# Loads of x asked for earlier, and a scheduling model with two kinds of DMA queue, in a hybrid decoder layer

## What is computed

```python
h = x
h = h + parallel_mixer(rms_norm(h, mix_norm_g), ...)          # this stage is where the change lies
h = h + memory_cross_attention(rms_norm(h, cross_norm_g), ...) # 4 heads into 256 memory tokens
h = h + swiglu_ffn(rms_norm(h, ffn_norm_g), ...)               # width 2816
# in parallel_mixer
proj = xn @ w_in                                   # 1024 -> 3072
q, k, v, u = split(proj, [1536, 2048, 2560])       # q: 3 groups x 4 heads x 128; k, v, u: 512 each
q = rope_partial(rms_norm(q), cos, sin) * 128 ** -0.5
k = rope_partial(rms_norm(k), cos, sin)
# three dilated windows (128/1, 512/4, 2048/16) of q over k, v, merged by their denominators;
# u: causal means over 2, 4, 8, 16 positions minus the token, a linear map a group;
# both concatenated @ w_out
```

## Time and profile before

| | |
|---|---|
| median of three runs | 1014.95 us |
| profiled execution | 1013.88 us |
| its slowest core (core 1), first to last instruction | 1012.3 us |
| spans of cores 0 to 7 | 1008.2, 1012.3, 1011.8, 1004.5, 1005.1, 1010.1, 998.9, 1011.2 us |
| granted TensorE clock of cores 0 to 7, mean share | 0.991, 0.993, 0.993, 0.993, 0.995, 0.991, 0.998, 0.993 |
| PE busy on core 1 | 953.9 us, 94% of the span |
| DVE, ACT, POOL busy | 446.1, 386.1, 170.5 us |
| chain that ended last | 88% PE, 4% DMA, 2% DVE, 2% ACT |

### The profile page before, as it was taken

How to read it: one execution, slowest core, us unless ns; L and a number is a source line. 1 busy time by engine, 2 the same in 40 slices (tenths; PEclk the granted TensorE clock), 3 DMA queues, 4 the chain that set the end, 5 groups by cost and what they waited for, 6 DMA issues and landing times.

```text
span 1012.3 us, 16727 instructions; the slowest of 8 cores (998.9 to 1012.3 us)
## 1 busy us (share of the span) xinstructions
PE 953.9 (94%) x5716; PEld 474.3 (47%) x5716; DVE 446.1 (44%) x970; ACT 386.1 (38%) x726; POOL 170.5 (17%) x253
## 2 busy tenths in 40 slices
PE   1789999999998799989999999999999999999998
PEld 1345545555556575434443444444444444444443
DVE  2437793666774457656787221122261212211111
ACT  2436656555558785436784111112110111111000
POOL 1214453333340002111220000010110000010000
PEclk9989999999999999999999999999999999999999
DMA  9876434020039779400220345448476255539471
GB/s 220 207 139 162 116 54 77 14 51 12 11 101 182 226 214 194 114 0 1 37 48 1 47 79 84 84 74 125 97 130 138 42 84 84 83 61 138 80 143 59
DMA packets 65587, 96.45 MB, mean 95 GB/s; under 512 B 27616, under 2 KB 38752, under 8 KB 63328
## 3 DMA queue, kind: packets, MB, share of 16 engines
q0 software_dynamic: 28496, 50.96, 32.5%
q1 hardware_dynamic: 19968, 40.09, 12.5%
q10 hardware_dynamic: 17040, 4.33, 2.0%
HBM read 133.74 MB, written 12.58 MB: 145 GB/s over the span
## 4 chain that ended last, share of the span: by engine, by line
PE 88%; DMA 4%; DVE 2%; ACT 2%; issue 2%; ACTq 1%; POOL 0%; SPq 0%; DVEq 0%; POOLq 0%
PE psall L306 86%; DMA arena<-v_scr 3%; ACT arena L317 2%; PE psall L309 2%; DMA arena<-xt 1%; DVE arena L335 1%; ACTq L352 1%; DVE arena L324 1%; DVE arena L339 0%; DVE arena L329 0%; POOL arena L324 0%; ACT L317 0%; DVE arena L346 0%; SPq L352 0%; DVEq L203 0%
## 5 line engine op out<-in xcount | busy, mean ns | idle before, releaser
L306 PE MATMUL psall<-arena 128*128 128x512 bf16 (+4 forms) x5396 | 943.1, 335 | 51.4 <-DMA arena<-xt 14.8
L306 PEld LDWEIGHTS psall<-arena 128*128 128x128 bf16 x5396 | 454.2, 100 | 517.9 <-issue 87.0
L317 ACT ACTIVATE arena<-psall 128x512 bf16<-128x512 f32 (+4 forms) x350 | 226.1, 670 | 321.6 <-PE psall L306 295.7
L324 POOL TENSOR_TENSOR arena<-arena 128x256 f32<-128x256 bf16 (+5 forms) x192 | 124.7, 661 | 334.4 <-DVE arena L335 160.1
L324 DVE TENSOR_TENSOR arena<-arena,psall 128x512 bf16<-128x512 f32 x88 | 60.5, 688 | 238.9 <-PE psall L306 235.0
L317 ACT ACTIVATE arena<-arena 128x512 f32<-128x512 f32 (+5 forms) x292 | 114.8, 410 | 125.0 <-DVE arena L324 67.2
L324 DVE TENSOR_TENSOR arena<-psall,arena 128x512 f32<-128x512 f32 (+1 forms) x128 | 86.4, 687 | 149.7 <-PE psall L306 144.9
L335 DVE SCALAR_TENSOR_TENSOR arena<-psall,arena 128x128 bf16<-128x128 f32 (+2 forms) x372 | 111.2, 357 | 58.4 <-ACT arena L317 29.4
L324 DVE TENSOR_TENSOR arena<-arena 128x1024 bf16<-128x1024 bf16 (+3 forms) x86 | 57.9, 676 | 42.2 <-ACT arena L317 31.0
L339 DVE TENSOR_REDUCE arena<-arena 128x4 f32<-128x512 bf16 x80 | 54.0, 681 | 48.6 <-ACT arena L317 48.5
L355 POOL DMA_DIRECT2D arena<-w_gu_t x22 | 16.5, 753 | 290.6 <-PE psall L306 290.6
(11 more groups left out here) (14 smaller groups left out, 15.7 us busy)
## 6 DMA issues: line engine op xcount, KB each, us to landing
arena<-w_gu_t POOLq DMA_DIRECT2D x22, 1024.0 KB, 8.6
arena<-w_in_t SPq DMA_DIRECT2D x12, 1024.0 KB, 7.9
arena<-w_d_t POOLq DMA_DIRECT2D x8, 1408.0 KB, 18.0
arena<-xr SPq DMA_DIRECT2D x4, 2048.0 KB, 13.0
outT<-arena SPq DMA_DIRECT2D x32, 256.0 KB, 4.0
arena<-xt POOLq DMA_DIRECT2D x7, 1024.0 KB, 12.1
v_scr<-arena ACTq DMA_DIRECT2D x32, 128.0 KB, 2.7
arena<-v_scr SPq DMA_DIRECT2D x4, 1024.0 KB, 8.0
```

The costliest lines, as they stand in the source:

```text
L306: P.op("pe", lambda e: e.matmul(out, lhsT=lhsT, rhs=rhs, start=start, stop=stop), r, w, max(0.056, 0.003 + size(out) / 2400))
L317: P.op("act", lambda e: e.activation(out=out, in_=in_, func=func, **kw), r, w, 0.18 + 0.00085 * size(out))
L324: P.op(eng, lambda e: e.tensor_tensor(out=out, in0=in0, in1=in1, op=op), r, w, dcost(eng, size(out), per))
```

## The change

Three edits. (1) The first tiles of x: the loads of x2 and x3 no longer wait for x0 and x1; the load of tiles 4 to 7, which waited for x2, becomes two loads of two tiles without a wait; the load of tiles 8 to 11, hung on k's unit of tile 4, becomes two of two tiles, hung on v's units of tiles 1 and 3. (2) The two halves of chunk 3 (q0's weights), hung on k's units of tiles 5 and 7, are now hung on that of tile 8 and wait for the landing of x11. (3) The model of `order` has two buses, one for POOL's DMAs and one for those of SP and ACT. A DMA of POOL starts 3.5 us after its issue; where the other bus is taken it moves at 90 GB/s (POOL) or 190 GB/s, else at 240 in place of 210; the latency is 2.0 in place of 2.2 us. Nothing else differs in the text; the order of any engine's list can.

```diff
@@ def order(self):
-        SEM, DMA_LAT, BW = 0.12, 2.2, 210e3
+        SEM, DMA_LAT, BW, SHARE = 0.12, 2.0, 240e3, {"pool": 90e3, "hw": 190e3}
-        bus = 0.0
+        bus = {"pool": 0.0, "hw": 0.0}
...
             if o.is_dma:
-                bus = max(bus, free[e]) + o.nbytes / BW
-                o.end = bus + DMA_LAT
+                q, other = ("pool", "hw") if e == "pool" else ("hw", "pool")
+                t0 = max(bus[q], free[e] + (3.5 if e == "pool" else 0.0))
+                beside = max(0.0, bus[other] - t0)
+                if beside * SHARE[q] >= o.nbytes:
+                    bus[q] = t0 + o.nbytes / SHARE[q]
+                else:
+                    bus[q] = t0 + beside + (o.nbytes - beside * SHARE[q]) / BW
+                o.end = bus[q] + DMA_LAT
...
-        load_x(2, 1, r=[("x", 0)])
-        load_x(3, 1, r=[("x", 1)])
+        load_x(2, 1)
+        load_x(3, 1)
         load_w(1, 0, r=[("ws", 0)])
         load_w(1, 1, r=[("ws", 1)])
-        load_x(4, 4, r=[("x", 2)])
+        load_x(4, 2)
+        load_x(6, 2)
...
-                ("k", 4): [lambda: load_x(8, 4)], ("k", 6): [lambda: load_x(12, 4)], ("k", 9): [lambda: load_x(16, 4)],
-                ("k", 5): [lambda: load_w(3, 0)], ("k", 7): [lambda: load_w(3, 1)],
+                ("v", 1): [lambda: load_x(8, 2)], ("v", 3): [lambda: load_x(10, 2)], ("k", 6): [lambda: load_x(12, 4)], ("k", 9): [lambda: load_x(16, 4)],
+                ("k", 8): [lambda: load_w(3, 0, r=[("x", 11)]), lambda: load_w(3, 1, r=[("x", 11)])],
```

## The result

| | before | after |
|---|---|---|
| median of 11 runs each, taken in turns on one chip | 1014.15 us | 1001.71 us |
| ratio after/before, 95% interval | | 0.9877 (0.9857 to 0.9898) |
| profiled execution | 1013.88 us | 1000.78 us |
| its slowest core | core 1, 1012.3 us | core 0, 999.2 us |
| mean of the eight cores' spans | 1007.8 us | 993.1 us |

What follows compares the result with a forecast made beforehand. PE's fixed matmul work was taken to bound the kernel, with most removable loss before 66.9 us. Terms 3.8 + 0 + 6.9 + 0 = 10.7 us gave 1003.2, or 1004 on the median; range 998 to 1014.5 (forecast's own 1001 to 1007).

Steps and rivals of the forecast that it cites:

- (c): From 49 us, v's stores hold ACT; PE's 4.1 us wait and 2.8 us of low clock would go: 6.9 us.
- (b): PE's small waits for POOL and DVE after (a): left at 4.6 us; term 0, between -3 and +3.
- the later stages: Work the model reorders from 66.9 us on, mostly PE's idle time after 303 us: 0, between -3 and +3.
- (a): 14.8 to 27.4 us: weights scaled late; new order cuts PE's 7.1 us waits to 3.3, gaining 3.8 (0 to 6).
- ACT does the Sins and the scaling before 14 us: Sign of being right: Sins and two scalings stand on ACT before 14 us, while PE waits for x0.
- The count by what is outstanding: Stores of v4 onward: v8 sticks from 57 us to about 61 to 65; ACT loses 4 to 8 us.
- just fits: Store of v7, issued at 53 us: 109 to 116 packets an engine outstanding, so it should not stick.
- short gaps before x8 and x12 let them flush: no stick: Stores of v0 to v3, about 31 to 37 us, clear the queue in gaps between x loads; gives the 6.9 us.
- R1: Stall moves to v7 and v8, (c) returns nearly whole: only 4 us won, 1011 us; chance 0.20.
- R2: No gap before x12: stores stick from v4 to about 66 us; 4 to 7 us slower, 1020; chance 0.13.
- The fixed cost of a load: Splitting x4 to x11 into pairs: quoted 2.0 us per DMA, 4.0 for two more; prediction took no cost.
- The bound of some 115 packets an engine: ACT's store queue: about 115 packets an engine can be outstanding, so a fourth v store's issue sticks.

Runs made afterwards that it cites:

- e2_loads: Kernel after with the old one-bus model, so the loads' half of the change alone: 1024.21 us, ratio to before 1.0089.
- e1_model: Kernel before with only the new two-bus model of `order`, every load asked for as before: 998.01 us, ratio to before 0.9822.
- e6_xwait: Kernel after with the old waits of x2 and x3, and x4 to x7 as one load waiting for x2: 1001.46 us, ratio to before 0.987.
- e10_late: Kernel before with the old model up to model time 200 us and the new one from there: 1007.7 us, ratio to before 0.9923.
- e7_before_fewpk: Kernel before with v's stores as 128 rows of 1 KB a tile (v permuted, for timing only): 1009.36 us, ratio to before 0.9921.
- e8: Kernel after with q1's two weight halves waiting for x15: 1000.25 us, ratio to before 0.9839.
- e4_fewpk: Kernel after with v's stores as 128 rows of 1 KB a tile (v permuted, for timing only): 990.39 us, ratio to before 0.9745.
- e5_sp: Kernel after with v's stores of tiles 0 to 11 issued by SP instead of ACT: 988.34 us, ratio to before 0.9727.
- e9_model_sp: Kernel before with the new model and v's stores of tiles 0 to 11 issued by SP, old loads: 994.59 us, ratio to before 0.976.
- e3: Kernel after with q0's weight halves back on k's units of tiles 5 and 7, not waiting for x11: 1001.35 us, ratio to before 0.9857.

## Why the prediction was right, and where it was not

**The time** was forecast at 1004 us and is 1001.7. The way there was half right, and that the time fits is luck: (c) missed by over 10 us, and (b) and the later stages, for which nothing was forecast, made up for it.

*(a) The order of the first scaling: right.* Forecast 3.8 us; PE's idle time up to 30 us fell from 6.9 to 2.6, by 4.3. As forecast, ACT does the Sins and the scaling before 14 us. That the model does it is shown by e2_loads, which has the change's loads and the old model: 6.7 us of idle time, as before. With the new model it is 2.6 to 3.0 us in seven kernels; only in e1_model it is 4.6, for x and for one wait for DVE L335 of 2.7 us, and e6_xwait with x2 and x3 as late has 3.0, so the early loads aren't what (a) needs.

*(b) The small waits: mis-sized.* I left them at 4.6 us, "since DVE, ACT and POOL have as much work in less time". They went from 4.9 to 0.1 us (30 to 56 us), 4.8 us more than the term gave, and beyond its bound of 3. Old order: 4.6 to 5.7 us (before, e10, e7, e2). New order: 0.1 to 0.8 (after, e6, e8, e4, e5, and e9 with all loads as before); in e1 and e3 there are 4.2 and 7.1 us, mostly for x. They were waits of order, not of load.

*(c) What holds ACT: failed.* The step that fell everywhere is a wait that the count left out, at nothing and without a reason: before its issue a store on ACT waits for the landing of the fourth store before it, as there are four semaphores. The count by what is outstanding came true on cores 1, 4, 5, 6 and 7: v7 "just fits" (its issue takes 0.4 us) and v8's issue sticks, for 1.6 to 5.4 us. But v8 could not be issued before v4 had landed, at 64.5 to 71.8 us, and ACT waited 7.5 to 13.8 us for that. On cores 0, 2 and 3 a step before it fell as well, "short gaps before x8 and x12 let them flush: no stick": v3, issued at 38.1 us on core 0, landed at 65.2, as x12 to x15 were asked for at 37.77 us and q0's weights ran beside them, and the stick comes at v6 already, at 49.77 us, 8.8 to 11.8 us long. ACT loses 13.9 us in all on the mean core (8.3 and 5.6), where 4 to 8 were forecast; in the kernel before it is 9.5.

The idle time from 56 to 110 us went from 4.1 to 9.0 us. The time at the low clock before 110 us went from 7.7 to 9.4 us, but it cost no more than before: PE's busy time up to A, which holds what a low clock costs, fell from 270.0 to 268.8 us (265.9 in e4_fewpk, which has no low clock before 110 us). In place of +6.9 the term gave -4.9 + 1.2 = -3.7 us. It is R1, the stall moves, at a price between R1's, where (c) is about 0, and R2's, where it is -8 or worse. The time of R1 didn't come only because (b) and the later stages paid. e7_before_fewpk shows the cost in the kernel before to be about what I took; e4_fewpk and e5_sp show what taking it away would have brought here, 13 and 15 us by the ratios.

*Later stages: mis-sized.* I took 0, between -3 and +3, on the ground that "the order of work there hangs on loads issued long ahead". The change gave 7.8 us after A on the mean core; e10_late, which has only this, gives 10.4 us there and is 7.8 us faster on the slowest core. 25.8 us of PE's idle time lay after 303 us, more than in the first 70 without the first tile, and the prediction doesn't say of any of it what released it. The four waits near 436 us, all for DVE or ACT, were there to be read.

*The fixed cost of a load.* x4, x5 landed at 27.96 us and x6, x7 at 31.55, 3.6 us apart for 1 MB of source; that is nearer to half of the 6.0 us for 2 MB than to that half with the fixed cost that the prediction quotes (2.0 us) added. e6_xwait, with one load for the two, takes the same time. Taking 0 was right.

Together, means of the eight cores: 4.3 + 4.8 - 4.9 + 1.5 (idle after 110 us, 1.8 to 0.3) = 5.7 us of waits, and 1.2 us of PE's busy time: A moved by these 6.9 us. The first wait for x has no part in it (13.7 us in both). With 7.8 behind A that makes 14.7 on the mean core. The slowest core sets the time: in the kernel after it lies 6.1 us over the mean (999.2 and 993.1), before 4.5 (1012.3 and 1007.8), so the profiled executions differ by 13.1 and the medians by 12.4.

## What to carry to other kernels

In a kernel like this one, a DMA of many small packets should not be issued by an engine that computes while large loads run on other queues: ACT was held by its stores for 14 us here, partly in the issue and partly for the landing of an earlier one whose semaphore was to be used again; rearranging the loads only moved the wait, and issuing the stores from SP, or with a quarter of the packets, ended it. So count both the packets that are outstanding and the semaphores. And look at all cores: the slowest one showed a form of this stall that five of the eight didn't have. When a hand-made scheduling model is changed, its effect must be looked for in every stage where PE idles behind DVE or ACT, not only where the model's new constants speak of DMA. And two edits made together should be run apart: here one gave all of the gain and the other cost a part of it.

## What the runs showed of the hardware

- An issue sticks on SP as on ACT (one of 9.4 us on SP in e9_model_sp; two in 13.86 on ACT in e2_loads, one in 8.78 in the kernel after), and with a quarter of the packets it doesn't (0.33 us). The bound of some 115 packets an engine, worked out ahead of the change, was measured by no run by itself. Counted in the same way, 33 packets a store less those that had left q10 when the sticking issue ended, it is 132 - 19 = 113 in e1_model, 132 - 23 = 109 in e2_loads and 112 for v8 on core 1 of the kernel after, but 231 - 134 = 97 for v6 on its core 0: an estimate, and not one fixed number.
- With three queues at work each gets one packet in turn, whatever the size: 205 packets of weights moved 1.55 MB, while 201 of the stores moved 0.05 MB.
- In e1_model ACT also sticks, 6.6 us from 41.3 us on core 3, and PE pays almost nothing for it (0.7 us from 56 to 110 us). It waits 3.73 us for x at the same time; that this hides the stick is likely, not shown:

```profile
44.54 14.39 PE L312 MATMUL psall<-arena 128*128 128x128 bf16 x72 [3.73 <-DMA arena<-xt]
```

- Left open: in the kernel after, the even cores end attention at 402 to 406 us and the odd ones at 394 to 397, 8.5 us apart in the mean, while at A they are 2.8 us apart (296.2 and 293.4). The slowest core is an even one (spans 999.2, 996.6, 995.6, 998.3 against 989.3, 989.9, 986.9, 989.3 us). No experiment was aimed at it.
